# The last norm taken in halves, the first block of x rounded by VectorE, and the convolution's first gate and tap on ScalarE

## The reference

```python
def rmsnorm(x, g):
    y = xf * lax.rsqrt(jnp.mean(xf * xf, axis=-1, keepdims=True) + NORM_EPS)
    return (y * g.astype(jnp.float32)).astype(x.dtype)

def short_conv_mixer(h, w_in, conv_w, w_out):
    gate_b, gate_c, v = jnp.split(h @ w_in, 3, axis=-1)
    z = gate_c * v
    zp = jnp.pad(z, ((0, 0), (1, 1), (0, 0)))
    zc = conv_w[0] * zp[:, :-2] + conv_w[1] * zp[:, 1:-1] + conv_w[2] * zp[:, 2:]
    return (gate_b * zc) @ w_out
...
for i in range(DEPTH):                     # DEPTH = 2
    h = rmsnorm(x, norm_mix[i])
    x = x + (short_conv_mixer(...) if i == 0 else neighborhood_attention_2d(...))
    h = rmsnorm(x, norm_mlp[i])
    x = x + sqrelu_mlp(h, w_up[i], w_down[i])
return rmsnorm(x, norm_final)
```

## Time and profile before

| | |
|---|---|
| median of 3 runs | 1039.65 us (1038.97 to 1040.02) |
| the profiled execution | 1039.44 us, of which 1037.3 us are the span of the profile |
| PE busy | 1028.6 us, 99% |
| DVE busy | 842.0 us, 81% |
| ACT busy | 599.2 us, 58% |
| POOL busy | 105.1 us, 10% |
| chain that ended last | PE 95%, DVE 3%, DMA 1%, ACT 1% |

### The profile page before, as it was taken

The page is one execution under the profiler, slowest core; times in us unless marked ns, Lnnn a source line. Parts: engine busy times, 40 slices in busy tenths (PEclk is TensorE's granted clock), DMA queues, the critical chain, the costliest instruction groups (busy, mean ns, idle before and its releaser), DMA issues.

```text
span 1037.3 us, 15366 instructions
## 1 busy us (share of the span) xinstructions
PE 1028.6 (99%) x6088; PEld 903.3 (87%) x6088; DVE 842.0 (81%) x1173; ACT 599.2 (58%) x837; POOL 105.1 (10%) x160
## 2 busy tenths in 40 slices
PE   9999999999999999999999999999999999999997
PEld 7888888988998998998888888889888988988985
DVE  4497788699899689688997667797899798698697
ACT  6221356565584574575775555656664774674675
POOL 0347101000000000001013000000000000000003
PEclk9999999999999999999999999999999999999999
DMA  8798979226745645633998733166056547447423
GB/s 325 141 397 288 292 204 251 84 50 224 205 131 163 186 130 172 175 99 97 372 263 238 212 106 111 43 213 253 1 127 208 163 133 202 149 134 202 148 51 112
DMA packets 37110, 182.97 MB, mean 176 GB/s; under 512 B 5808, under 2 KB 5936, under 8 KB 22960
## 3 DMA queue, kind: packets, MB, share of 16 engines
q1 hardware_dynamic: 23184, 108.57, 29.8%
q0 software_dynamic: 13568, 72.91, 28.4%
q10 hardware_dynamic: 288, 0.52, 0.2%
HBM read 137.20 MB, written 27.33 MB: 159 GB/s over the span
## 4 chain that ended last, share of the span: by engine, by line
PE 95%; DVE 3%; DMA 1%; ACT 1%; issue 0%; POOL 0%; POOLq 0%; ACTq 0%; DVEq 0%
PE bank L769 30%; PE bank L770 30%; PE bank L771 30%; PE bank L974 2%; PE bank L952 1%; PE bank L937 1%; DVE w_l L1508 1%; DMA raw<-weights 1%; PE bank L792 1%; DVE big L1947 0%; PE bank L996 0%; DVE hx L1953 0%; DVE a_l L1721 0%; ACT big L1167 0%; ACT big L1144 0%
## 5 line engine op out<-in xcount | busy, mean ns | idle before, releaser
L1116 ACT ACTIVATE w_h<-big 128x1024 fp32r<-128x1024 f32 x210 | 221.7, 1058 | 216.2 <-PE bank L771 215.5
L769 PE MATMUL bank<-a_h,w_h 128*128 128x256 f32 (+1 forms) x892 | 294.4, 330 | 0.3 <-DVE w_l L1508 0.3
L771 PE MATMUL bank<-a_h,w_l 128*128 128x256 f32 (+1 forms) x892 | 292.8, 328 | 0.0
L770 PE MATMUL bank<-a_l,w_h 128*128 128x256 f32 (+1 forms) x892 | 292.8, 328 | 0.0
L1508 DVE TENSOR_TENSOR w_l<-big,w_h 128x1024 fp32r<-128x1024 f32 x210 | 252.1, 1227 | 21.8 <-ACT w_h L1116 21.8
L769 PE MATMUL bank<-w_h,hx 128*128 128x512 f32 x568 | 221.8, 391 | 0.0
L770 PE MATMUL bank<-w_l,hx 128*128 128x512 f32 x568 | 221.1, 389 | 0.0
L771 PE MATMUL bank<-w_h,hx 128*128 128x512 f32 x568 | 221.0, 389 | 0.0
L769 PEld LDWEIGHTS bank<-a_h,w_h 128*128 128x128 f32 x892 | 169.6, 190 | 16.0 <-issue 0.5
L771 PEld LDWEIGHTS bank<-a_h,w_l 128*128 128x128 f32 x892 | 169.6, 190 | 15.0
L770 PEld LDWEIGHTS bank<-a_l,w_h 128*128 128x128 f32 x892 | 169.6, 190 | 14.4
(11 more groups left out here) (189 smaller groups left out, 1243.3 us busy)
## 6 DMA issues: line engine op xcount, KB each, us to landing
big<-blocks SPq DMA_DIRECT2D x56, 1024.0 KB, 5.0
big<-big POOLq DMA_DIRECT2D x30, 1024.0 KB, 7.7
raw<-weights SPq DMA_DIRECT2D x52, 512.0 KB, 8.5
raw<-t_sums SPq DMA_DIRECT2D x16, 512.0 KB, 3.6
t_sums<-sevens POOLq DMA_DIRECT2D x6, 1024.0 KB, 13.7
t_sums<-t_sums POOLq DMA_DIRECT2D x6, 1024.0 KB, 12.5
raw<-sevens SPq DMA_DIRECT2D x12, 512.0 KB, 7.0
bias_tiles<-big POOLq DMA_DIRECT2D x8, 632.0 KB, 9.8
```

Of the source, the lines that this page charges most:

```text
L769: nc.tensor.matmul(dst, sh, mh, start=start, stop=False, skip_group_check=again)
L770: nc.tensor.matmul(dst, sh, ml, start=False, stop=False, skip_group_check=again)
L771: return nc.tensor.matmul(dst, sl, mh, start=False, stop=stop, skip_group_check=again)
L1116: nc.scalar.activation(wh_all[:, w % SLOTS, :], src, ACT.Copy).then_inc(w_hi, 1)
```

## The change

At the start, DVE instead of ACT rounds block 0 of x, ahead of its other work. `par` is issued by ACT behind `wave[0]`, so that SP begins with x. PE runs six matmuls of constants where it ran eight, and block 1 gets matmuls of its own, as block 0 has, in the order high by high, low x, low weights.

In the convolution, C is copied from its bank by ACT, and DVE multiplies v's bank by that copy; the product is scaled once by `rstd2`, the square of `rstd`, which is why DVE no longer needs `rstd` for its first gate. The first tap is ACT's. These 16 ACT instructions stand behind the `hi` of the units in `GATE_BEHIND` and `TAP_BEHIND`. The two lists `LO_BEHIND_GATE` and `LO_BEHIND_Z` place DVE's `lo`.

At the end, tile t = 3 is computed in two column halves of 256, in two banks, and added and squared by halves. The result for t = 0 is DVE's, one instruction of 128x1024, ahead of its adds for P7. ACT's scaling of t = 1 stands behind two of its squares. The chain of small DVE instructions from the root to the inverse root has one less.

```diff
+GATE_BEHIND = (7, 9, 10, 11, 12, 14, 16, 18)
+TAP_BEHIND = (9, 10, 11, 12, 14, 15, 17, 19)
+LO_BEHIND_GATE = (None, 10, 11, 12, 13, 15, 16, 18)
+LO_BEHIND_Z = (9, None, None, None, 14, None, 17, None)
...
+        last_half = [bank[3][:, 0:256], bank[6][:, 0:256]]
...
         def _(sp):
-            sp.dma_start(par[:], small).then_inc(par_in, 16)
...
+                        for c, dst in enumerate(last_half):
+                            cols = slice(256 * c, 256 * c + 256)
+                            for k in range(4):
...
+                                last = three(dst, xh[:, k, P:2 * P], xl[:, k, P:2 * P], wh[:, k % 2, cols], wl[:, k % 2, cols],
+                                             k == 0, k == 3, True)
+                            if c == 0:
+                                last.then_inc(tile_done, 1)
...
-            for _ in range(8):
+            for _ in range(6):
                 nc.tensor.matmul(bank[5][:, 0:P], ones[:], ident[:], start=True, stop=True)
             pe.wait_ge(piece_hi, 1)
-            pe.wait_ge(a_hi, 1)
+            pe.wait_ge(first_hi, 1)
...
+            def last_means(cell, at, before, half_before):
+                nc.vector.scalar_tensor_tensor(out=nrm[:, 0, at], in0=sqa[:, 3, cell, at], scalar=1.0 / D, in1=before,
+                                               op0=ALU.mult, op1=ALU.add).then_inc(var_ready, 1)
+                link(nc.vector.scalar_tensor_tensor(out=eps[:, 2, at], in0=sqa[:, 3, cell, at], scalar=-0.5 / D,
+                                                    in1=half_before, op0=ALU.mult, op1=ALU.add))
+            def last_inverse(t, cell):
+                at = slice(t, t + 1)
+                dve.wait_ge(sq_acc, SQ_LAST + {2: 5, 3: 7}[t])
+                link(nc.vector.scalar_tensor_tensor(out=nrm[:, 1, at], in0=sqa[:, 3, cell, at], scalar=-0.5 / D, ...
+                dve.wait_ge(std_ready, 7 + t)
+                link(nc.vector.reciprocal(nrm[:, 3, at], nrm[:, 2, at]))
+                link(nc.vector.scalar_tensor_tensor(out=nrm[:, 4, at], in0=nrm[:, 3, at], scalar=nrm[:, 1, at], ...
+                nc.vector.scalar_tensor_tensor(out=nrm[:, 5, at], in0=nrm[:, 4, at], scalar=1.5, in1=nrm[:, 3, at], ...
...
             dve.wait_ge(par_in, 16)
+            dve.wait_ge(x_in[0], 16)
+            nc.vector.tensor_scalar(a_h[:, 0, :], xT[:, 0, :], gain(0, 0), None, ALU.mult).then_inc(first_hi, 1)
...
-                scaled(w, w % 8, ev[0])
...
-                scaled(w + 1, (w + 1) % 8, ev[1])
...
-                link(nc.vector.tensor_tensor(zp[:, 8:520], ev[0], ev[1], ALU.mult))
+                nc.vector.tensor_tensor(ev[1], bank[(w + 1) % 8][:], ev[0], ALU.mult).then_inc(taken, 2)
...
+                link(nc.vector.tensor_tensor(zp[:, 8:520], ev[1], rstd2, ALU.mult))
...
-                link(nc.vector.tensor_scalar(ev2[0], zp[:, 0:512], tap(0, m), None, ALU.mult))
```

206 lines of the change are left out of this document (131 added, 75 removed).

## The result

The changed kernel takes 1042.10 us in the median of 12 runs (1040.07 to 1043.15), the kernel before 1039.86 on the same chip (12 runs, 1038.97 to 1041.7). The ratio is 1.0021, 95% interval 1.0014 to 1.0028: 0.2% slower, above the forecast and outside its range; slower by 2.1 us or more had been given 0.05. The profiled execution took 1042.03 us.

A forecast was written before the change was run, and what follows sets the result against it. PE, busy 1028.6 of 1037.3 us, was taken as the bound. Span 1037.3 - 0.4 (start) + 0 (convolution) + 0.3 (tail) = 1037.2, plus 2.1 around it, 1039.3; predicted median 1039.5 us, 8 in 10 for 1038.3 to 1040.9.

The forecast's parts named there:

- slower by 2.1 us or more: Whole kernel: chance 0.05 of being slower by 0.2%, against 0.91 for within and 0.04 for faster.
- `par` goes behind `wave[0]`, ... it is there at 3.5, or, if it queues behind `wave[0]`, at some 3.9: Start: `par`, issued on ACT's queue at about 1.17 us, lands 2.3 us later, or at some 3.9 if queued.
- nothing below, if `par` is late by 1 us: Start: lower bound of the gain, no gain at all if `par` lands 1 us late.
- the clock rises later: Rival, start: fewer constants or a gap delay PE's full clock, 1.1 us lost, 1041.0 us in all; chance 0.1.
- the constants end when x is ready: Start: the argument against a later clock rise; constants end at 4.5 us, when real matmuls start.
- a rise at 6.3 as before: Start: PE's clock assumed to go from 1.2 to 2.4 GHz at 6.3 us, unchanged, giving a gain of 0.5.
- the 0.4 of the sum: Start: the gain taken from real matmuls starting 0.9 to 0.95 us earlier, partly at the low clock: 0.4 us.
- The convolution: Convolution: 9 us less DVE work worth 0, 16 added ACT instructions cost 0, new waits hidden from PE.
- The tail: After PE's last matmul: last results start at 1033.75, not 1033.46, so the tail is 0.3 us longer.
- the tail does what it shows: Rival, tail: t = 3's add follows PE and the tail gives 0.7 us, 1038.5 us in all; chance 0.2.
- POOL going first: Rival, tail: POOL's multiplication goes ahead of DVE's result at 1024.70, tail 1.28 us longer, 1040.8 us; chance 0.05.
- PE in the middle: Rival: PE waits in the convolution or at its one weight wait, each us costs one, 1042 us; chance 0.05.

The follow-up runs named there:

- e13_spare_first: The changed kernel plus a 32 KB transfer that nothing reads, first on SP's queue ahead of x's block 0: 1041.12 us, ratio 1.0014 to the kernel before.
- e12_spare_second: The changed kernel plus a 32 KB transfer that nothing reads, on SP's queue between x's blocks 0 and 1: 1041.33 us, ratio 1.0011 to the kernel before.
- e1_par_sp: The changed kernel with `par` alone moved back to first place on SP's queue: 1039.42 us, ratio 1.0002 to the kernel before.
- e2_warm12: The changed kernel with twelve constant matmuls in place of six: 1041.22 us, ratio 1.0014 to the kernel before.
- e4_start_only: The kernel before with all the change's edits of the start, none of the convolution or tail: 1042.02 us, ratio 1.0025.
- e5_conv_only: The kernel before with the change's edits of the convolution alone: 1039.94 us, ratio 1.0002.
- e6_tail_only: The kernel before with the change's edits of the last norm alone: 1040.33 us, ratio 1.0005.
- e9_tail2: `e1_par_sp` with the tail reordered: earlier POOL multiplications and ACT scaling of first halves, DVE's t = 0 result cut to 512 columns and later: 1039.27 us, ratio 0.9992.
- e10_best7: `e9_tail2` with seven constants instead of six: 1038.98 us, ratio 0.9988 to the kernel before.
- e8_par_sp_second: The changed kernel with `par` on SP's queue between x's blocks 0 and 1: 1039.98 us, ratio 1.0004 to the kernel before.

## Why the prediction was wrong

**The start: the step that failed** is "`par` goes behind `wave[0]`, ... it is there at 3.5, or, if it queues behind `wave[0]`, at some 3.9". It was there at 5.99. The 2.3 us were read from a row in which `par` was the first transfer of all, and the move was priced as a change of queue only. The move back alone gives back the loss (1039.42), the move alone makes it (1042.51). The move does two more things. It makes `par` one of the last of four: with that alone it landed at 4.5 and 4.7 (`e13_spare_first`, `e12_spare_second`). And it makes SP's queue shorter, so that x's block 1 goes out at 1.2 us instead of 1.6, beside the three that PE waits for: this is the rest, to 5.99. I had counted the earlier issue of x's block 0 (0.4 us) as a gain and did not follow the queue to the next transfer. The bound "nothing below, if `par` is late by 1 us" named the right transfer, but it was late by 2.1 to 2.5 us.

**The clock: right as a mechanism, too small and too unlikely.** The rival "the clock rises later" has its gap, and its price, 1.1 us, is about what six constants alone cost the kernel before (1040.75 for 1039.66, though the interval of the ratio begins at 0.9999). But I gave it 0.1, since "the constants end when x is ready", and let "a rise at 6.3 as before" stand though the gap in front of it was new. Nor was 6.3 a fixed time: with the start of before, block 0 ended at 8.59, 8.72 and 9.30 us in three traces. That it ended 0.43 earlier in `e1_par_sp`, as the 0.4 of the sum, is luck: there all of it ran at full rate. The late start, 6.65 behind a gap of 2.0 us, came on top. Of the 2.2 us between the medians, `e2_warm12` gives back 0.7 as the gap's; the 1.5 that it keeps are the 1.3 of its block 0 and 0.3 to 0.5 of tail, less up to 0.3 us of weight wait. The granted clock of the page reads full speed here as before; the cadence shows the level of 1.2 GHz for about seven matmuls of the changed kernel (four in 2.05 us, three of the four in 1.58), where before it was two. The Trainium skill (TensorE: Matmul & The Clock Gate, Part 1) says that it is not a number of matmuls that lifts the clock, and that the rise varies from run to run. The traces agree with both: seven real matmuls against two, and none in `e4_start_only`, behind the changed kernel's gap of 2.0 us.

**The convolution: right.** The gate copy, the tap at 51.68 and the rounding at 52.31 lie where the two lists put them (52.2), PE never waits, and `e5_conv_only` measures nothing. DVE's busy time fell by 7.6 us in `e5_conv_only` (842.0 to 834.4, forecast 9) and was worth nothing, as forecast.

**The tail: right in its order, short by 0.2 us.** Predicted 0.3 longer, 0.51 by the link in the changed kernel's trace, 0.4 in `e1_par_sp` and 0.6 in `e6_tail_only`. Take 2.26 off the rows of after: the adds begin at 1025.94 (predicted 1025.98), t = 1's result at 1028.50 (1028.5), t = 2's square at 1029.54 (1029.6). Then t = 2's root comes at 1030.61 and not at 1030.4; this slip of 0.2 goes through to the end (last root 1032.92 for 1032.67, last results 1033.97 for 1033.75). In `e1_par_sp` and `e6_tail_only` that root came as forecast (5.8 us behind the link) and the 0.1 to 0.3 us were lost between it and the inverse root. What held them is not shown. The rival "the tail does what it shows" (1038.5) fell in this order of instructions, but its thought was good: with another order (`e9_tail2`, `e10_best7`) the last results start 8.52 us behind the link, 0.4 us earlier than before. These versions move DVE's result and POOL's work at once, so which of the two it is stays open.

**POOL.** DVE went first at the link, as chosen, and POOL's first multiplication then took 2.33 us for 512 columns, where the earlier trace rows has 1.28: it was held while DVE's result with two SBUF inputs ran (1.28 us), and gave it back on DVE's next small instruction with two such inputs (0.78 us, 0.7 counted). The Trainium skill (GPSIMD Engine Reference, Specifications) says that the two contend for their SBUF interfaces when the DVE instruction has two SBUF inputs. These rows agree: POOL lost 1.05 us, and beside DVE's adds, which read a bank, it lost nothing (2.56 for two). The prediction had this only as a price for POOL going first; here DVE went first and POOL paid.

**PE in the middle.** The one wait of the earlier trace rows did not grow but vanished. It is also absent in `e6_tail_only`, which starts as before, so this is chance and not the later PE.

**Left open:** why a transfer issued 0.4 us later can slow one on the same queue that is ahead of it (x's block 0, 4.1 us, for 3.2 and 3.5 in `e8_par_sp_second` and `e12_spare_second`, where it also starts beside `wave[0]`), and why the engines together move less for it. The Trainium skill (DMA: Bandwidth & Descriptors, Queues, rings and completion order) says that each engine takes turns between the queue rows it has work for; by that, block 1 behind block 0 on SP's queue would cost block 0 nothing, and the landings above do not agree. Open too is why `e1_par_sp` and `e13_spare_first`, with equal gaps, differ (ratios 1.0002 and 1.0014); 11 times each are few for a mixture of two groups.

## What to carry to other kernels

Moving a small transfer from one queue to another moves all that stand behind it on the old one: list each bulk transfer with its new time of issue, and price the first operands by a row with as many in flight, not by the row in which they were alone. A warm-up that ends before the operands come can cost more than the gap, and costs it in some executions only, so fit it to the latest operand and look at the single times, not at the median alone. And between VectorE and GpSimd, which held each other up here, a result given to the one that seems idle can be paid by the other's next instruction: put it where neither is on the path.

## What the runs showed of the hardware

- With two 256 KB transfers issued by 1.2 us, a 32 KB one issued with or behind them landed 2.1 to 3.5 us after its issue; with three, one behind `wave[0]` took 4.7 to 4.8 us. In second place, SP's queue or ACT's made at most 0.3 us of difference (3.2 on SP's, 3.3 and 3.5 on ACT's).
- The six constants of the kernel before end 0.5 us ahead of block 0 and its times leave 1.4 us empty between two groups (1039.30, 1040.73). Block 0, which starts at 5.15 to 5.17 us, ended at 8.16 in one version's trace and at 9.96 in another's. Without a gap the time at which TensorE leaves its lower clock varied too, but less: with the start of before, block 0 ended at 8.59, 8.72 and 9.30.
- With a third transfer of 256 KB issued by 1.2 us, the DMA engines together moved less up to 3.5 us (0.28 to 0.44 MB) than with two (0.47 to 0.53 MB).
- A GpSimd multiplication (128x512, two SBUF inputs) of 1.29 us took 2.33 beside a VectorE instruction of 1.28 us with two SBUF inputs, and a VectorE one of 0.2 us took 0.78 behind a GpSimd one.
